# Block 1 modulation rows: full-width row blocks of w_ada into four PSUM banks, and ten small loads moved to another queue

## The reference, cut to what matters

```python
mods = jax.nn.silu(c) @ w_ada + b_ada                 # c: (1, 1024), w_ada: (1024, 6144)
shift1, scale1, gate1, shift2, scale2, gate2 = jnp.split(mods[:, None, :], 6, axis=-1)
h = rms_norm(x, norm1_g) * (1.0 + scale1) + shift1    # x: (1, 256, 1024)
proj = h @ w_in                                       # w_in: (1024, 3360)
y_rwkv = rwkv7_time_mix(proj[..., :RWKV_PROJ], ...)   # uses the LoRA weights w_up, a_up, g_up
y_moba = moba_attention(proj[..., RWKV_PROJ:], ...)
x = x + gate1 * (concat([y_rwkv, y_moba]) @ w_out)
h = rms_norm(x, norm2_g) * (1.0 + scale2) + shift2
x = x + gate2 * moe_ffn(h, w_router, b_router, w_gate_up, b_gate_up, ...)
```

## Time and profile before

| | us |
|---|---|
| median of 3 runs | 1598.03 (1597.63 to 1599.55) |
| the profiled execution | 1597.56 |
| its span, first to last instruction | 1595.8 |
| mean granted TensorE clock | 0.990 of full |

### The profile page before, as it was taken

One profiled execution on the slowest core, in us unless ns is written; L12 is line 12 of the kernel. 1 busy time (PEld: TensorE's weight loads), 2 busy tenths in 40 slices (PEclk: granted clock), 3 DMA queues, 4 the chain that ended last, 5 costly groups with the idle time before them and its releaser, 6 DMA issues.

```text
span 1595.8 us, 20357 instructions
## 1 busy us (share of the span) xinstructions
PE 1508.4 (95%) x8382; PEld 778.6 (49%) x8383; DVE 369.3 (23%) x712; ACT 285.0 (18%) x451; POOL 34.5 (2%) x86
## 2 busy tenths in 40 slices
PE   5999899999999998999999989989999999999998
PEld 3885687733333333333333333333333885888443
DVE  2475442412121211111112112112111233301003
ACT  2123312211111111111111111111111232100000
POOL 5000110000000000000000000000000000000000
PEclk9999999899999999999999999999999999999999
DMA  9865204789999999999999999999999641444420
GB/s 347 293 235 213 77 3 177 301 341 426 430 428 428 428 427 427 431 429 428 427 427 430 430 428 427 427 430 430 428 427 412 245 149 62 159 158 159 158 106 27
DMA packets 75038, 503.23 MB, mean 315 GB/s; under 512 B 5278, under 2 KB 8496, under 8 KB 50416
## 3 DMA queue, kind: packets, MB, share of 16 engines
q1 hardware_dynamic: 72240, 498.22, 76.2%
q10 hardware_dynamic: 2752, 4.34, 0.8%
HBM read 501.49 MB, written 1.05 MB: 315 GB/s over the span
## 4 chain that ended last, share of the span: by engine, by line
PE 70%; DMA 25%; DVE 3%; ACT 1%; ACTq 1%; issue 0%; SPq 0%; DVEq 0%
DMA ring<-in_w_gate_up 24%; PE psum L1105 16%; PE psum L1141 9%; PE psum L1351 6%; PE psum L1366 5%; PE psum L634 5%; PE psum L1173 3%; PE psum L1054 3%; PE psum L559 2%; PE psum L1038 2%; PE psum L972 2%; PE psum L1308 2%; PE psum L1376 2%; PE psum L1098 1%; PE psum L681 1%; PE psum L1323 1%
## 5 line engine op out<-in xcount | busy, mean ns | idle before, releaser
L1105 PE MATMUL psum<-ring,work 128*64 128x512 f32 x2048 | 457.5, 597 | 44.2 <-DMA ring<-in_w_gate_up 44.2
L1105 PEld LDWEIGHTS psum<-ring,work 128*64 128x64 f32 x2048 | 140.5, 137 | 359.8 <-issue 270.0
L1141 PE MATMUL psum<-ring,work 128*64 128x512 f32 x1024 | 226.8, 595 | 1.6
L2121 DVE TENSOR_SCALAR work<-psum 128x512 f32<-128x512 f32 x32 | 22.1, 692 | 629.0 <-PE psum L1105 629.0
L1141 PEld LDWEIGHTS psum<-ring,work 128*64 128x64 f32 x1024 | 71.3, 137 | 136.4 <-issue 130.0
L1633 ACT ACTIVATE work<-work 128x512 f32<-128x512 f32 x32 | 20.1, 629 | 445.5 <-DVE work L2121 445.5
L1351 PE MATMUL psum<-xT,ring 128*128 128x256 f32 x448 | 96.9, 379 | 0.0
L1351 PEld LDWEIGHTS psum<-xT,ring 128*128 128x128 f32 x448 | 85.0, 190 | 11.5
L1366 PE MATMUL psum<-ring 128*128 128x512 f32 x192 | 82.6, 592 | 0.0
L634 PE MATMUL psum<-hT,ring 128*128 128x256 f32 (+1 forms) x368 | 80.4, 380 | 1.1 <-DMA ring<-in_w_in 1.1
L634 PEld LDWEIGHTS psum<-hT,ring 128*128 128x128 f32 (+1 forms) x368 | 68.3, 186 | 13.3 <-ACT hT L1443 1.3
(11 more groups left out here) (432 smaller groups left out, 1259.5 us busy)
## 6 DMA issues: line engine op xcount, KB each, us to landing
ring<-in_w_gate_up SPq DMA_DIRECT2D x128, 2048.0 KB, 32.0
ring<-in_w_down SPq DMA_DIRECT2D x72, 2048.0 KB, 35.3
ring<-in_w_ada SPq DMA_DIRECT2D x12, 2048.0 KB, 12.8
ring<-in_w_up SPq DMA_DIRECT2D x8, 2048.0 KB, 7.6
ring<-in_w_in SPq DMA_DIRECT2D x6, 2048.0 KB, 8.6
ring<-in_w_out SPq DMA_DIRECT2D x4, 2048.0 KB, 7.7
ring<-in_w_in_sb SPq DMA_DIRECT2D x4, 2048.0 KB, 22.8
ring<-in_w_mem_kv SPq DMA_DIRECT2D x1, 2048.0 KB, 9.1
```

The source lines that it names most:

```text
L1105: ins = mm(B(1 + u)[CAP * h:CAP * (h + 1), :], xe[:, k % 4, k // 4, :], w[:, k % 2, c0:c0 + 512], start=False, stop=k == KT - 1)
L1141: last = mm(B(3)[CAP * h:CAP * (h + 1), :], act[:, k % 4, k // 4, :], w[:, k % 4, 512 * h:512 * (h + 1)], start=k == 0, stop=k == KT - 1)
```

## The change

The first four loads of w_ada are no longer 512 columns of all rows, but 256 rows with all 2048 columns (rows of 8 KB and not of 2 KB). The same number of matmuls now writes four banks in parallel; the accumulation over k goes on over the four loads. The transposes and sums are replaced by one-column matmuls with `id4`, which has ones in rows 0, 32, 64 and 96 of its column 0, into bank 1. ScalarE copies banks 0 and 5, VectorE banks 4 and 6. The ten loads behind the parameters leave ScalarE's queue: four LoRA loads go behind "in" 1 on SyncE's queue, and six loads of router and bias rows behind "in" 3. GpSimd builds `id4` before `pool_stage` 2. Counts of semaphores are renumbered (not shown).

```diff
@@ prologue loads (SyncE)
-                if kind == "ada":
+                if kind == "ada" and i < 4:
+                    load(ada_rows(s), a["w_ada"][0, 2 * P * i:2 * P * (i + 1), 0:2048].rearrange("(k p) n -> p k n", p=P),
+                         S(f"pro_in{s}"))
+                elif kind == "ada":
                     load(slot8(s), chunk_cols(a["w_ada"][0], 512 * i, 512), S(f"pro_in{s}"))
...
+                if n == 5:
+                    load(wl[0:LOW, 0, :], a["rwkv_w_up"][0], S("wl_in"))
+                    load(wl[LOW:P, 0, :], a["rwkv_a_up"][0], S("wl_in"))
+                    load(wl[:, 1, :], a["rwkv_g_up"][0, 0:P, :], S("wl_in"))
+                    load(wl[0:GLOW - P, 2, :], a["rwkv_g_up"][0, P:GLOW, :], S("wl_in"))
+                if n == 9:
+                    load(w_rout[:, :, :], a["w_router"][0].rearrange("(k p) n -> p k n", p=P), S("rout_in"))
+                    load(b_rout[:, :], a["b_router"], S("rout_in"))
+                    for q in range(4):
+                        load(bgu[E_N * q:E_N * (q + 1), :], a["b_gate_up"][0, :, 512 * q:512 * (q + 1)], S("bgu_in"))
@@ GpSimd: in front of pool_stage 2, no longer behind it
+            ch.link(g_.memset(id4[:, :], 0.0))
+            for q in range(4):
+                ch.link(g_.affine_select(out=id4[:, :], in_=id4[:, :], pattern=[[-1, E_N]], base=-E_N * q,
+                                         channel_multiplier=1, compare_op=ALU.not_equal, fill=1.0))
@@ TensorE
-            for n in range(5):
-                if n < 4:
-                    arrived(n)
-                    if n >= 2:
-                        pe.wait_ge(S("ada_copied"), n - 1)
-                    w = slot8(pro_slot(n))
-                    for k in range(KT):
...
+            for n in range(4):
+                arrived(n)
+                w = ada_rows(pro_slot(n))
+                parts = [(kk, cg) for kk in range(2) for cg in range(4)]
+                if n == 3:
+                    parts.sort(key=lambda x: x[1])
+                for at_, (kk, cg) in enumerate(parts):
+                    k = 2 * n + kk
+                    q = 32 * (k % 4)
+                    last = mm(B(ADA_BANK[cg])[q:q + 32, :], silc[:, k, :], w[:, kk, 512 * cg:512 * (cg + 1)],
+                              start=k < 4, stop=k >= 4)
+                    if n == 3 and kk == 1:
+                        last.then_inc(S("ada_groups"), 1)
+                    elif at_ % 4 == 3:
+                        last.then_inc(S("halves_used"), 1)
+            for cg in range(4):
+                pe.wait_ge(S(["ada_copied", "ada_copied_d"][cg % 2]), cg // 2 + 1)
+                for j in range(4):
+                    last = mm(B(1)[:, 4 * cg + j:4 * cg + j + 1], ada_sb[cg][:, j * P:(j + 1) * P], id4[:, 0:1],
+                              start=True, stop=True)
+                    if cg == 3 and j in (1, 2):
+                        last.then_inc(S("halves_used"), 1)
+            last.then_inc(*mark("mod_rows"))
@@ ScalarE: the ten dma(...) of L1416 to L1423 are gone
-            for n in range(4):
-                ac.wait_ge(S("halves_used"), 2 * n + 2)
-                if n >= 2:
-                    ac.wait_ge(S("ada_turned"), n - 1)
-                A(ada_sb[n % 2], B([0, 4][n % 2]), ACT.Copy).then_inc(S("ada_copied"), 1)
+            for cg in (0, 2):
+                ac.wait_ge(S("ada_groups"), cg + 1)
+                A(ada_sb[cg], B(ADA_BANK[cg]), ACT.Copy).then_inc(S("ada_copied"), 1)
@@ VectorE
-            for n in range(4):
-                ada_sum(n, 5 + n % 2)
-            ve.wait_ge(S("ada_summed"), 4)
-            ch.link(V.tensor_tensor(mods[:, 0:16], mods[:, 0:16], par[:, 0:16], ALU.add))
+            for cg in (1, 3):
+                ve.wait_ge(S("ada_groups"), cg + 1)
+                V.tensor_copy(ada_sb[cg], B(ADA_BANK[cg])).then_inc(S("ada_copied_d"), 1)
+            ve.wait_ge(*at("mod_rows"))
+            ch.link(V.tensor_tensor(mods[:, 0:16], B(1)[:, 0:16], par[:, 0:16], ALU.add))
```

More of the change, by code:

```diff
@@ L65 @@
     "tensor": [
-        "par_turned", "xss", "lora_w", "lora_a", "lora_g", "kkss", "bonss", "qkss", "vturned",
+        "par_turned", "xss", "mod_rows", "lora_w", "lora_a", "lora_g", "kkss", "bonss", "qkss", "vturned",
         "biki_turned", "shift_0", "shift_1", "wsh_spread", "logits", "ranks", "wt_turned",
@@ L250, in build @@
         silc = silc_t[:, :, :]
-        ada_sb = [view(ws, 8192 + 512 * i, [512]) for i in range(2)]
+        ada_sb = [view(ws, 7168 + 512 * i, [512]) for i in range(4)]
         ada_late = view(tok_f, 0, [512])
@@ L317, in halves_before, with ada_rows @@
             return 2 * sum(not on_dve(x) for x in range(n))
-        def pe_ada(x):
-            return x if x < 4 else x - 5
+        def ada_rows(s):
+            return ring[:, s, :].rearrange("p (k n) -> p k n", k=2)
+        ADA_BANK = [0, 4, 5, 6]
         def pro_slot(n):
@@ L475, in _ @@
                 ch.link(g_.memset(praw[b][:, :, 0:1], 0.0))
+            ch.link(g_.memset(id4[:, :], 0.0))
+            for q in range(4):
+                ch.link(g_.affine_select(out=id4[:, :], in_=id4[:, :], pattern=[[-1, E_N]], base=-E_N * q,
+                                         channel_multiplier=1, compare_op=ALU.not_equal, fill=1.0))
             g.sem_inc(S("pool_stage"), 1)
             ch.link(g_.memset(blk[:, :], 0.0))
-            ch.link(g_.memset(id4[:, :], 0.0))
             ch.link(g_.memset(rev_tri[:, :], 1.0))
@@ L493, in select @@
                                         compare_op=op, fill=fill))
-            for q in range(4):
-                select(id4[:, :], [[-1, E_N]], -E_N * q, 1, ALU.not_equal, 1.0)
             ch.link(g_.memset(blk[0:HD, 0:HD], 1.0))
@@ L768, in ada_turn @@
             def ada_turn(x, bank):
-                pe.wait_ge(S("ada_copied"), pe_ada(x) + 1)
+                pe.wait_ge(S("ada_copied"), x - 6)
                 for j in range(4):
@@ L1012, in _ @@
             pe.wait_ge(*at("shift_out"))
-            pe.wait_ge(S("ada_summed"), 5)
+            pe.wait_ge(S("ada_summed"), 1)
             second_norm(0)
@@ L1071, in _ @@
             pe.wait_ge(*at("npass_ready"))
-            pe.wait_ge(S("ada_summed"), 7)
+            pe.wait_ge(S("ada_summed"), 3)
             pe.wait_ge(*at("wtT_ready"))
@@ L1415, in _ @@
             assert n_dma == N_PAR_DMA
[L1416 to L1423, removed]
             for n, b in enumerate((4, 6)):
@@ L1773, in ada_sum @@
             def ada_sum(n, bank):
-                ve.wait_ge(S("ada_turned"), pe_ada(n) + 1)
+                ve.wait_ge(S("ada_turned"), n - 8)
                 turned = B(bank).rearrange("p (j q r) -> p j q r", j=4, q=4)
                 V.tensor_reduce(mods[:, 4 * n:4 * n + 4], turned[:, :, :, 0], AX.X, ALU.add).then_inc(S("ada_summed"), 1)
-            for n in range(4):
-                ada_sum(n, 5 + n % 2)
-            ve.wait_ge(S("ada_summed"), 4)
-            ch.link(V.tensor_tensor(mods[:, 0:16], mods[:, 0:16], par[:, 0:16], ALU.add))
+            for cg in (1, 3):
[3 more added lines that the diff above has]
+            ch.link(V.tensor_tensor(mods[:, 0:16], B(1)[:, 0:16], par[:, 0:16], ALU.add))
             V.scalar_tensor_tensor(out=sc1[:, :], in0=mods[:, 8:16], scalar=1.0, in1=col("norm1_g", 0, 8),
@@ L1993, in _ @@
             ada_sum(9, 2)
-            ve.wait_ge(S("ada_summed"), 5)
+            ve.wait_ge(S("ada_summed"), 1)
             ch.link(V.tensor_tensor(mods[:, 36:40], mods[:, 36:40], par[:, 36:40], ALU.add))
@@ L2098, in _ @@
             ada_sum(11, 7)
-            ve.wait_ge(S("ada_summed"), 7)
+            ve.wait_ge(S("ada_summed"), 3)
             ch.link(V.tensor_tensor(mods[:, 40:48], mods[:, 40:48], par[:, 40:48], ALU.add))
```

## The result

| | before | changed |
|---|---|---|
| median | 1598.79 us (1597.63 to 1600.43, 4 runs) | 1612.11 us (1609.28 to 1614.71, 4 runs) |
| profiled execution, span | 1597.56, 1595.8 | 1611.07, 1609.3 |

The ratio is 1.0075 with a 95% interval of 1.0061 to 1.0089: 13.3 us slower between the medians, 13.5 between the profiled executions. Predicted were 1611.7 us and +13.7.

The account below looks back on a forecast made before the run. Bound: the chain up to the projection's start at 39.24 us, with TensorE fully busy from there. Four terms moved that start to 52.9, +13.7 us, giving 1611.7 us; range 1597 to 1616, the forecast's own 1608 to 1615.

Parts of the forecast that it names:

- term 1: TensorE's wait for the last parameter transfer, beside the w_ada stream in 8 KB packets: ends at 25.9 us, not 13.73.
- term 2: Sum of squares after the parameter transposes: 16 instructions, 5.86 us, much of it at half clock, from 26.4 to 32.3.
- term 3: Modulation products on w_ada: two wide in place of four, 33 x 0.427 = 14.1 us, from 32.3 to 46.4.
- term 4: Last product to projection: turning 3.5 us, then bias, `sc1`, h and start 2.9; 6.5 us in all, projection at 52.9.
- 45 to 55 turns: Parameter transfers on q10: packet turns needed on the DMA engine that has most of them, one for one with q1.
- the window of four: TensorE's products: look-ahead spans four unstarted instructions, so a group of eight costs four places, 33 places in all.
- what was said to be covered: Hidden before and after the projection: "in" 0 by 6.7 us, LoRA loads, six loads behind "in" 3, GpSimd's five instructions.
- the shadow of the parameter wait: Before the squares: ScalarE, free at 9.17 us instead of 15.3, gains nothing; with early parameters up to 4.4 us.

Follow-up runs that it names:

- rows_2k: The changed kernel with each of its first four w_ada loads cut into four transfers of 512 columns, 2 KB packets; ratio 1.0019 to the kernel before.
- rows_4k: The changed kernel with each of its first four w_ada loads cut into two transfers of 1024 columns, 4 KB packets; ratio 1.0030 to the kernel before.
- hold_8k: The changed kernel, but SyncE waits for the last parameter transfer before issuing the second of four w_ada loads; 1605.84 us, ratio 1.0036 to the kernel before.
- rotate_groups: The changed kernel with a product's column group q = 32*((k + cg) % 4), not 32*(k % 4); 1610.91 us, ratio 1.0054 to the kernel before.
- after_again: The same program as the changed kernel, measured again; ratio 1.0091 to the kernel before.
- loads_back: The changed kernel with the ten small loads back on ScalarE's queue behind the parameters; ratio 1.0126 to the kernel before.

## Why the prediction was right

Its four terms against the profile after:

| | predicted | measured |
|---|---|---|
| term 1, the wait ends | 25.9 | 24.59 |
| term 2, products start | 32.3 | 31.36 |
| term 3, products | 14.1 | 14.11 |
| term 4, to the projection | 6.5 | 6.30 (45.47 to 51.77) |
| projection | 52.9 | 51.77 |
| end against before | +13.7 | +13.5 |

Term 1 is right in mechanism (rows_2k, rows_4k, hold_8k) and 1.3 us too long, and two errors partly cancel in it. I had the parameters end with the stream, at 25.3. The stream's last packet ended at 26.29, 1.0 us later; the last small packet on q10 ended at 24.09, 2.2 us before it. From the end of x (10.29 on q10) that is 13.8 us, or 42 turns of 0.33 us, where I had 45 to 55 turns. x itself took 0.46 us a turn as priced, but began at 2.90 us and not at 3.4.

Term 2: 6.14 us from 25.22 to 31.36 against 5.86. The clock was at half as assumed, though not throughout: the instructions start 0.43 us apart until 30.1 and 0.22 us apart after that. Term 3 is right in size, 14.11 against 14.1, and right in that runs of eight on one group leave TensorE two wide. Its exactness is luck: it has 32 places of 0.436 us, where I had 33 of 0.427, and the window of four that gave the 33 does not hold in rotate_groups. The rule of the Trainium skill that matmuls start in program order ("TensorE: Matmul & The Clock Gate", Part 3: Packing small matmuls) is contradicted by the fifth and ninth instruction starting together; by it the products would have taken 21.8 us. Term 4: the copies are hidden as said. The turning took 3.68 us for the 3.5 forecast and the rest 2.62 for 2.9; the 2.9, read from the kernel before, held 0.35 us of waiting for "in" 0.

Of what was said to be covered, "in" 0 was (no DMA wait at 51.77) and GpSimd's five instructions were. The DMA engines stood idle from 26.3 us until the next load was issued at 36.76, as forecast. The four LoRA loads took SyncE 3.4 us to issue (40.66 to 44.07) and not 2.1, and that was covered too: in the 48.2 us behind the projection TensorE ran 224 matmul instructions, as before. The later stretches are where the sum was helped by luck. The steps to the projection give +12.5, the end of the profiled execution +13.5. The missing 1.0 us is not one of my terms: 1.7 us arise in a stretch at half clock that the profile before does not have there (below), and some is given back later; where was not found. after_again has the same projection within 0.2 us, no such stretch at 112 us, others further on, and a span 3.1 us longer. So the agreement of 1611.7 with 1612.11 is better than the model earns; 12.5 us against 13.7 is its true error.

One sentence was wrong in what it suggests: that a free ScalarE "gains nothing, because it ends in the shadow of the parameter wait". Against the kernel before this holds, but loads_back shows that without the move the shadow would have been left by 5 us (the 4.67 us wait of the squares), and a queue held up would have been the next limit. I had priced the issue of the ten loads at its duration in the trace before, 6.1 us, though the change altered what drains that queue.

## What to carry to other kernels

Two queues that share the DMA engines take turns by the packet: before making one stream's packets larger, count the small transfers beside it that somebody waits for, and let them pass first (2 KB packets until they are through, or a wait as in hold_8k). When small-tile matmuls are reordered, put consecutive ones into different tiles of the array; TensorE looked past three waiting instructions of a group, so runs of eight on one group halved its width. Parts of one change should be timed singly: here a gain of 4 us was hidden by a loss four times its size.

## What the runs showed of the hardware that I had not expected

An issuing engine can be held while it issues: 14.56 us for a transfer of 128 bytes in loads_back, with ScalarE's arithmetic waiting behind it. SyncE shows it too, in the other direction. It issues the same 8 MB of w_ada in the kernel before (2 KB packets) and in the changed one (8 KB packets):

```profile
0.80 14.87 SPq L347 DMA_DIRECT2D ring<-in_w_ada  x4
...
0.80 2.25 SPq L349 DMA_DIRECT2D ring<-in_w_ada  x4
```

With four times the packets the third load alone takes 6.17 us to issue, and 0.46 us in the changed kernel. That fits a queue that is full by its number of packets and not by their bytes; the limit itself was not measured.

TensorE's granted clock fell to half while TensorE was busy without a gap. In the changed kernel, 112.2 to 115.6 us and the stretch after it (PE, PEld, DVE, ACT, POOL, clock, DMA share, GB/s):

```profile
112.20:115.60 3.40, 3.40 (x5) 1.34 (x5) 0.00 (x0) 2.26 (x3) 0.00 (x0) 0.50 1.04 392
115.70:119.10 3.40, 3.40 (x17) 2.99 (x16) 2.33 (x2) 1.00 (x2) 0.00 (x0) 1.00 1.05 386
```

Before 112.2 it had been busy since 51.77. Such stretches lie elsewhere in each execution. The longest, in the profiled execution of rows_4k, is 27 us, again with TensorE fully busy:

```profile
236.00:263.00 27.00, 27.00 (x222) 23.16 (x223) 3.99 (x11) 3.96 (x7) 0.00 (x0) 0.50 0.00 1
```

That execution took 1614.79 us, others of the same kernel 1600.25 to 1614.34. They account for most of the spread of some 5 to 15 us between executions of one kernel here: rows_4k's four executions with a granted clock of 0.990 took 1601.71 to 1602.23 us, its three with 0.981 to 0.983 took 1610.17 to 1614.79. The clock also settles whether a shift of the projection moves the end one to one, as the prediction assumed. From the projection to the end the twelve profiled executions take 1556.3 to 1570.3 us, and 26.5 to 58.2 us of that are at half clock. Half of this time taken off, 1540.0 to 1543.3 us are left in all twelve. So the shift is passed on to within 3.3 us, and nearly all the rest is the clock.

What sets the stretches off was not found. The steps up to the projection repeated within 0.4 us in the two profiles of the changed kernel, but where such a stretch falls before the projection, as in rotate_groups and loads_back, it adds 1.7 to 1.8 us there too. For a change of a few microseconds at the start the place of a step in the profile, read together with the clock, tells more than the median does.
